# Wide products for all tiles of u, and one-hot rows of the gates from fp16 tables in PSUM

## The reference, cut to what matters

```python
def block(xc):                                   # 128 tokens of width 1024
    q = (xc @ w_q).reshape(PEER_CHUNK, PEER_HEADS, 2, half)
    sc = jnp.einsum('thpd,hpnd->thpn', q, subkeys).astype(jnp.float32)
    s1, i1 = lax.top_k(sc[:, :, 0], PEER_TOPK)
    s2, i2 = lax.top_k(sc[:, :, 1], PEER_TOPK)
    cand = (s1[..., :, None] + s2[..., None, :]).reshape(PEER_CHUNK, PEER_HEADS, ncand)
    cidx = (i1[..., :, None] * PEER_N_KEYS + i2[..., None, :]).reshape(PEER_CHUNK, PEER_HEADS, ncand)
    top, pos = lax.top_k(cand, PEER_TOPK)
    idx = jnp.take_along_axis(cidx, pos, axis=-1).reshape(PEER_CHUNK, PEER_HEADS * PEER_TOPK)
    gate = jax.nn.softmax(top, axis=-1).reshape(PEER_CHUNK, PEER_HEADS * PEER_TOPK)
    u_e = jnp.take(u, idx, axis=0)
    v_e = jnp.take(v, idx, axis=0)
    act = jax.nn.gelu(jnp.einsum('ted,td->te', u_e, xc).astype(jnp.float32))
    return jnp.einsum('te,ted->td', (gate * act).astype(v_e.dtype), v_e)
```

## Time and profile before

| | |
|---|---|
| Median of 3 runs | 2635.6 us |
| Lowest, highest | 2635.51, 2636.83 us |
| Span of the profiled execution | 2636.8 us |
| TensorE busy | 2599.8 us |
| VectorE busy | 1903.2 us |
| ScalarE busy | 1486.2 us |
| GpSimd busy | 709.0 us |
| Tiles of u of layer 0, first narrow one to the first product of v | 392.95 to 667.17 us |

### The profile page before, as it was taken

One profiled execution on the slowest core, in us unless ns is written; L12 is line 12 of the kernel. 1 busy time (PEld: TensorE's weight loads), 2 busy tenths in 40 slices (PEclk: granted clock), 3 DMA queues, 4 the chain that ended last, 5 costly groups with the idle time before them and its releaser, 6 DMA issues.

```text
span 2636.8 us, 41561 instructions
## 1 busy us (share of the span) xinstructions
PE 2599.8 (99%) x15917; PEld 2295.5 (87%) x15917; DVE 1903.2 (72%) x3327; ACT 1486.2 (56%) x2420; POOL 709.0 (27%) x354
## 2 busy tenths in 40 slices
PE   9999999999999999999999999999999999999998
PEld 7888889999888887778899998888878888998887
DVE  5667799888666667877998886666678767756784
ACT  4443567778555454655677875554454457543543
POOL 0001787777100002015886773000010021100000
PEclk9999999999999999999999999999999999999999
DMA  6555555454666665345655556666645656213564
GB/s 235 161 174 185 168 188 180 154 160 154 206 193 193 195 194 191 115 146 167 191 181 158 159 154 199 208 193 195 195 158 188 191 171 185 71 65 120 177 191 160
DMA packets 124996, 452.49 MB, mean 172 GB/s; under 512 B 13936, under 2 KB 14064, under 8 KB 124800
## 3 DMA queue, kind: packets, MB, share of 16 engines
q1 hardware_dynamic: 122832, 442.62, 53.1%
q0 software_dynamic: 1968, 7.22, 0.9%
HBM read 447.68 MB, written 2.10 MB: 171 GB/s over the span
## 4 chain that ended last, share of the span: by engine, by line
PE 93%; DVE 4%; issue 1%; ACT 1%; DMA 0%; POOL 0%; SPq 0%; DVEq 0%; POOLq 0%; ACTq 0%
PE ps L651 14%; PE ps L681 11%; PE ps L683 11%; PE ps L682 11%; PE ps L625 7%; PE ps L648 7%; PE ps L626 7%; PE ps L627 7%; PE ps L668 2%; PE ps L670 2%; PE ps L669 2%; DVE W L1758 2%; PE ps L799 2%; PE ps L941 1%; PE ps L787 1%
## 5 line engine op out<-in xcount | busy, mean ns | idle before, releaser
L1241 ACT ACTIVATE hi<-ring 128x1024 fp32r<-128x1024 f32 x830 | 866.4, 1049 | 211.2 <-PE ps L683 106.5
L2677 POOL TENSOR_TENSOR ring_r<-ring,hi 128x1024 fp32r<-128x1024 f32 x260 | 623.1, 2407 | 1131.3 <-ACT hi L1241 1131.1
L1788 DVE TENSOR_TENSOR ring_r<-ring,hi 128x1024 fp32r<-128x1024 f32 x570 | 696.8, 1228 | 256.1 <-ACT hi L1241 254.6
L625 PE MATMUL ps<-xT_r,hi 128*128 128x256 f32 x1560 | 453.0, 290 | 1.0 <-DVE ring_r L1788 1.0
L626 PE MATMUL ps<-xT_r,hi 128*128 128x256 f32 x1560 | 440.4, 282 | 0.0
L627 PE MATMUL ps<-xT_r,ring_r 128*128 128x256 f32 x1560 | 440.2, 282 | 0.0
L681 PE MATMUL ps<-hi,oht_r 128*128 128x512 f32 x1040 | 404.8, 389 | 0.3 <-DVE oht_r L1758 0.2
L682 PE MATMUL ps<-ring_r,oht_r 128*128 128x512 f32 x1040 | 404.6, 389 | 0.0
L683 PE MATMUL ps<-hi,oht_r 128*128 128x512 f32 x1040 | 404.6, 389 | 0.0
L651 PE MATMUL ps<-xT_r,hi 128*128 128x512 f32 x1600 | 383.5, 391 | 0.0
L651 PEld LDWEIGHTS ps<-xT_r,hi 128*128 128x128 f32 x1600 | 293.5, 188 | 56.5
(11 more groups left out here) (299 smaller groups left out, 3621.7 us busy)
## 6 DMA issues: line engine op xcount, KB each, us to landing
ring<-in_peer_u SPq DMA_DIRECT2D x256, 512.0 KB, 3.5
ring<-in_peer_v SPq DMA_DIRECT2D x256, 512.0 KB, 4.2
ring<-in_f SPq DMA_DIRECT2D x132, 512.0 KB, 3.6
ring<-in_ret_vg SPq DMA_DIRECT2D x32, 512.0 KB, 3.6
ring<-in_peer_q SPq DMA_DIRECT2D x32, 512.0 KB, 3.6
ring<-in_ret_qk SPq DMA_DIRECT2D x16, 512.0 KB, 3.6
ring<-in_ret_out SPq DMA_DIRECT2D x16, 512.0 KB, 3.5
ring<-in_in_shift SPq DMA_DIRECT2D x14, 512.0 KB, 3.6
```

The costliest lines, as they stand in the source:

```text
L625: pe.matmul(o, h, xT[:, k, 0:256], start=k == 0, stop=False)
L1241: hid.done(a.activation(hi[m % NH][:, :], ring[j % NR][:, :], ACT.Copy), j)
L1788: lo_v.done(v.tensor_tensor(low_part[j % NR][:, :], ring[j % NR][:, :], as32(hi[m % NH][:, :]), ALU.subtract), j)
L2677: lo_p.done(p.tensor_tensor(low_part[j % NR][:, :], ring[j % NR][:, :], as32(hi[m % NH][:, :]), ALU.subtract), j)
```

## The change

1. All 128 tiles of u of a layer are wide products (`mat_w`), each in a bank of its own. `joined` for tiles from 64 on adds the halves of both tiles of a pair into the bank of the even one; the bank of the odd one is free then, that of the even one after `weigh`.
2. The gate stretch begins at tile 64 (before 62). Tiles 80, 100 and 112 (`TWO_GATES`) carry two gate steps.
3. The picks of all 256 tokens are kept as fp16 (index digits, and the gate in two parts), and transposed at tile 63 in eight fp16 transposes into bank 7, as two tables in which values of two tokens stand side by side. VectorE reads them there.
4. The one-hot rows of four tokens are made by two VectorE operations of 1024 columns: a comparison (`equal`) of `P_iota2`, the column numbers written twice each in fp16, and a multiplication (`hot`). The rows of two tokens alternate column by column, so TensorE reads both operands at a step of two. ScalarE has no part in it.
5. `low_half` and `gelu` on ScalarE, `gated`, `joined`, `weigh` on VectorE get a new order in the gate stretch; the ones are put into W by ScalarE alone, from tile 4 on; candidate and pick buffers move from W to `oht`, `selT` and `fzt`.

```diff
-PEER_A0 = 69
+PEER_A0 = 84
-GATE_TILE = 62
-U_WIDE = 44
+GATE_TILE = 64
+PICK_TILE = 63
+EXP_TILE = (27, 57)
+TWO_GATES = (80, 100, 112)
...
+        def tables(l):
+            t = psum[bank_of["peer_pick", l]].bitcast(F16).rearrange("p (w j z s) -> p w j z s", w=2, z=2, s=2)
+            return t[:, 0], t[:, 1]
...
+        GATES, _g = {}, 0
+        for _i in range(GATE_TILE, 128):
+            GATES[_i] = [g for g in range(_g, _g + 1 + (_i in TWO_GATES)) if g < 64]
+            _g += len(GATES[_i])
...
                 def gate(g):
                     b = bank("peer_g", l, g, among=B7)
-                    pe.wait_ge(*at(dve, "spread", l, g))
-                    pe.wait_ge(*at(act, "hot", l, g))
-                    hot = P_oh[g % 2]
-                    for s in range(4):
+                    pe.wait_ge(*at(dve, "hot", l, g))
+                    equal, hot = P_equal[g % 2], P_hot[g % 2]
+                    for t in range(4):
+                        j, q = t // 2, t % 2
                         for z in range(2):
-                            ins = pe.matmul(b[:, s * 128:s * 128 + 128], hot[:, s, 2, :], hot[:, s, 1 - z, :], start=z == 0, stop=z == 1)
+                            ins = pe.matmul(b[:, t * 128:t * 128 + 128], equal[:, j, 1, :, q], hot[:, j, z, :, q], start=z == 0, stop=z == 1)
...
+                for i in range(128):
+                    if i == PICK_TILE:
+                        bank("peer_pick", l, among=(7,))
+                        pe.wait_ge(*at(dve, "picks", l, 1))
+                        for tt in range(2):
+                            for z in range(4):
+                                ins = pe.transpose(tables(l)[z // 2][:, tt * 64:tt * 64 + 64, z % 2, :], P_picks[tt][:, z, :], P_ident)
+                        mm.done(ins, "peer_pick", l)
+                    mat_w(TILE["peer_u", l * 128 + i], None, "peer_u", l, i, among=B7)
+                    for g in GATES.get(i, ()):
+                        gate(g)
...
+            def joined(l, i):
+                v.wait_ge(*at(act, "low_half", l, i))
+                to = W[:, i * 256:i * 256 + 256]
+                if i >= GATE_TILE:
+                    to = ps("peer_u", l, i - i % 2)[:, i % 2 * 256:i % 2 * 256 + 256]
+                tt_(to, ps("peer_u", l, i)[:, 0:256], low_halves[i % 4], ALU.add, name=("joined", l, i))
+                if i < GATE_TILE or i % 2:
+                    empties(dve, "peer_u", l, i)
...
+                step(v.tensor_copy, P_iota2, b3(iota, [128, 128, 2], 2))
+                step(v.tensor_copy, P_ident, ident)
...
-                    if tt:
-                        picked(0)
-                        joined_by(1.8)
...
+                    stt_(e3, e3, GATE_SCALE, b3(second[:, 0:8], [128, 8, 16], 2), ALU.mult, ALU.mult)
+                    step(v.tensor_copy, P_picks[tt][:, 2, :], P_ev)
+                    tt_(P_picks[tt][:, 3, :], P_ev, P_picks[tt][:, 2, :], ALU.subtract, name=("picks", l, tt))
...
                 def one_hots(g):
+                    v.wait_ge(*(at(mm, "peer_g", l, g - 2) if g >= 2 else at(mm, "peer_pick", l)))
+                    index, gates = (z[:, g * 2:g * 2 + 2] for z in tables(l))
+                    equal, shape = P_equal[g % 2], [128, 2, 2, 128, 2]
+                    dve.done(v.tensor_tensor(equal, P_iota2.unsqueeze(1).unsqueeze(1).broadcast_to(shape), index.unsqueeze(3).broadcast_to(shape),
+                                             ALU.is_equal), "equal", l, g)
+                    v.wait_ge(dve.sem, dve.n)
+                    dve.done(v.tensor_tensor(P_hot[g % 2], equal[:, :, 0].unsqueeze(2).broadcast_to(shape), gates.unsqueeze(3).broadcast_to(shape),
+                                             ALU.mult), "hot", l, g)
...
+                for i in range(GATE_TILE, 127):
+                    for g in GATES[i]:
+                        gated(g)
+                        if g == GATES[i][0]:
+                            joined(l, i)
+                        if g < 62:
+                            one_hots(g + 2)
+                    if not GATES[i]:
+                        joined(l, i)
+                    if i % 2 == 0 and i > GATE_TILE:
+                        weigh(i - 2)
```

More of the change, by code:

```diff
@@ L800, in gate @@
                     mm.done(ins, "peer_g", l, g)
[L802 to L810, removed]
-                        for j in range(i, i + 2):
-                            mat_w(TILE["peer_u", l * 128 + j], None, "peer_u", l, j, among=B7)
-                        continue
-                    g = i - GATE_TILE
-                    mat_t([TILE["peer_u", l * 128 + i + j] for j in range(2)], None, "peer_u", l, i, among=B7,
-                          behind=(lambda j: gate(g + j)) if 0 <= g < 64 else None)
+                for i in range(128):
[9 more added lines that the diff above has]
+                        gate(g)
@@ L1396, in peer @@
                 prep(1)
+                low_half(127)
                 gelu(126)
@@ L2062, in topk @@
                         joined_by(2.35)
-                        red_(P_picks[tt][z], eq, ALU.add)
+                        with nc.allow_low_precision(reason="an index is a whole number under 128"):
+                            red_(P_picks[tt][:, z, :], eq, ALU.add)
                         joined_by(2.35)
@@ L2114, in prep, with gated @@
                     dve.done(v.tensor_tensor(hi_part[:, 256:512], Wv[:, k, :], as32(hi_part[:, 0:256]), ALU.subtract), "prep", l, k)
-                one_hots(0)
-                one_hots(1)
-                step(v.memset, W[:, P_ONES[-1][1] * 256:], 1.0)
-                v.wait_ge(*at(act, "ones", l))
-                v.wait_ge(*at(act, "gelu", l, GATE_TILE - 2))
-                for g in range(64):
+                def gated(g):
                     wg = Wv[:, :, g * 4:g * 4 + 4]
@@ L2126, in peer @@
                     empties(dve, "peer_g", l, g)
-                    if g < 62:
-                        one_hots(g + 2)
-                    if g % 2 == 0 and g:
-                        weigh(GATE_TILE + g - 2)
-                empties(dve, "peer_iota", l)
-                for i in range(GATE_TILE + 62, 126, 2):
-                    weigh(i)
+                for i in range(first, GATE_TILE - 1):
+                    joined(l, i)
+                one_hots(0)
+                one_hots(1)
+                joined(l, GATE_TILE - 1)
+                v.wait_ge(*at(act, "ones", l))
+                v.wait_ge(*at(act, "gelu", l, GATE_TILE - 2))
+                for i in range(GATE_TILE, 127):
[6 more added lines that the diff above has]
+                    if not GATES[i]:
+                        joined(l, i)
+                    if i % 2 == 0 and i > GATE_TILE:
+                        weigh(i - 2)
+                empties(dve, "peer_pick", l)
                 prep(0)
                 prep(1)
+                joined(l, 127)
                 weigh(126)
@@ L2715, in peer @@
                     split(TILE["peer_u", l * 128 + i] + 2)
-                gains(l, 0, mm, "peer_u", l, 126)
+                gains(l, 0, mm, "peer_u", l, 127)
                 if l:
```

118 lines of the change are left out of this document (38 added, 80 removed).

## The result

The changed kernel takes 2748.8 us (median of 4 runs, 2747.2 to 2749.6) against 2636.1 us for the kernel before on the same chip: **1.0422 times as long, 95% interval 1.0410 to 1.0435, 112.6 us more.** The forecast was 2719 us, so the direction and the mechanism came out and some 29 us were missing. The profiled execution has a span of 2745.4 us.

A forecast was written before the change was run, and what follows sets the result against it. TensorE, busy 99% of the span, was taken to set the time. Net bank waits 72.0 us, late top-k 6.6 and clock 5 summed to 83.6 us on the 2635.6 us median, giving 2719 us, range 2698 to 2825.

The forecast's parts named there:

- Waits for banks: Gate stretch: TensorE waits 0.77 us at every second gate, 5.2 and 3.55 us around two-gate tiles; 43.9 us a layer.
- Narrow tiles to wide, with transposes and gates: u tiles: 84 a layer turn wide, saving 16.3 us in all; extra transposes cost 0.2 us a layer, gate matmuls nothing.
- Top-k late: Before tile 63's transposes: SBUF operations slowed beside GpSimd, 0 to 1.45 us each; 3.3 us a layer on path, 6.6 in all.
- Clock: TensorE's clock may drop after the 5.2 us waits: three drops of 1.7 us, 5 us taken, bounds 0 and 20.
- VectorE's steps from a gate's start to a free bank: Even gates: the bank is free 4.05 us after the gate's first matmul, while TensorE wants it after 3.28.
- the totals fit and do not decide: VectorE per gate and tile: 2.8 us of work against TensorE's 3.28 us fits, but totals do not decide.
- ScalarE's splitting as covered: Top-k stretch: exponentials hold up ScalarE's splitting of u, but it runs two tiles ahead of TensorE, more than the delay.
- The gate matmuls: TensorE's gates: reading both operands at a step of two changes nothing; cost bounded at 0.5 us a gate.
- Rival 3: Gate matmuls: strided weights load slowly, a gate takes 1.0 us instead of 0.5, +30 us a layer, 2780 us; 8%.
- 3.28 us for a gate and a tile: Gate stretch: TensorE takes 0.50 us for a gate plus 2.78 for a wide tile.
- rival 2: VectorE's one-hots run at one result per cycle, 1.21 us each, so waits grow 47 us a layer, 2813 us; 18%.
- rival 1: Gate stretch: no bank comes late, so the wide tiles' gain shows and the kernel is faster, 2620 us; 4%.

The follow-up runs named there:

- the eighth: Changed kernel with tiles and gates in separate banks, early table copies, and scaled gates written to PSUM (also listed as number 8): 2623.5 us, 0.9952 of the kernel before.
- Experiments 1: Changed kernel with VectorE's weigh of a pair moved ahead of the next even tile's gated: 2649.1 us, 1.0047 of the kernel before.
- experiment 2: Changed kernel with u tiles in banks 0 to 4 and gates in 5 and 6 from tile 64, nothing moved: 2640.3 us, 1.0012 of the kernel before.
- 5: Changed kernel with two gates at tile 80 alone, one each at tiles 100 and 112: 2707.6 us.
- experiment 6: Changed kernel without the second one-hot operation, the scaling by the gates, so its output differs: 2699.8 us.
- experiment 3: Changed kernel with idle TensorE transposes filling its six long waits of each layer: 2728.5 us, 20.2 us less.
- experiment 4: Changed kernel with the two table copies moved from the top-k's start into the queries' products: 2742.1 us, 6.7 us less.

## Why the prediction was right, and where 29 us were missing

| Term | Forecast | Measured |
|---|---|---|
| Waits for banks | +87.8 | +87.3 |
| Narrow tiles to wide, with transposes and gates | -15.9 | -12.8 |
| Top-k late | +6.6 | +14 |
| Clock | +5 | +23 |
| Sum | +83.6 | +111.5 |

The whole kernel shows +112.6; the last 1 us is in no row. The second row is measured as the way from the first product on u to the first on v in the kernel before (397.2 us in each layer) and in the eighth (390.8), where no wait of this change is left.

**The banks** were right to the half microsecond. Measured are 23 waits of 0.74 us, and three times 5.27 and 3.61 us a layer by the starts in the timeline (520.71 less 514.54 and 0.90 us for two gates; 532.28 less 528.23 and 0.44), 43.7 us against 43.9. For VectorE's steps from a gate's start to a free bank the prediction had 4.05 us: `weigh` ends 4.01 us behind the gate at 462.89, and the next gate starts 0.05 us later, 4.06 in all. Experiments 1 and 2 show it is the bank and nothing else, 5 and 6 that its size is the sum of those steps. Since the two engines wait for each other in turn, no busy share could show it; the forecast's remark that the totals fit and do not decide was the right one.

**The clock** is the step that failed, as a mis-sized term. The prediction saw that the waits of 5.2 us "could each bring" a drop, set 0 to 20 us, and took three drops of 1.7 us, 5 in all. Eleven of the twelve long waits brought one, five of the six of 3.4 us too, and experiment 3 puts them at 20.2 us, 1.7 for each of the twelve on the mean. That is the upper bound that the text had itself worked out from the earlier trace rows; the price of one drop was right, their number was not. No row spoke for three. Two more drops stand behind the waits at the transposes: from there to the first gate it is 7.46 and 7.60 us in the two layers, against 6.07 in both layers of the eighth kernel, which has neither wait nor drop there. That makes 2.9 us, and 23 in all.

**The top-k** was the other mis-sized term. The list of steps was right, and so was the mechanism, with its upper bound of 1.45 us for an operation: 8.7 us a layer. The value taken, 3.6, was near the middle of a range without a reason for the middle. In layer 0 the two copies cost 4.3 us too much and the cast and subtraction of the first half 2.2. Three of these four exceed the bound of 1.45 for one operation (the copies take 2.51 and 2.31 us, the subtraction 2.39, where some 0.3 would do), since an operation can wait for nearly the whole of a GpSimd instruction. From the first product on u to the transposes it is 182.4 us in each layer of the changed kernel and 175.5 in the eighth: 7.0 a layer, 14 in all. Of each 7.0 us, 4.2 are spent at the transposes, where the forecast had 3.3. The other 2.8 lie ahead of them, where the forecast had nothing: it named ScalarE's splitting as covered, since it runs two tiles ahead, and it was not. The waits for GpSimd at L663 came out of it, and experiment 4 removed them.

**The gate matmuls** cost no more with steps of two: eight take 0.63 us to the end of the last and 0.44 to the next start, against 0.62 and 0.43 before (542.61 to 543.04 in the kernel before). Rival 3 is out. The forecast's 3.28 us for a gate and a tile was 0.03 short of the 3.32 and 3.31 us that alternate in experiment 2. The forecast had taken the cost of a gate, 0.50 us, from narrow tiles; behind a gate a wide tile takes 2.88 us in place of 2.78, a narrow one 2.95 in place of 2.88. Over 128 gates this makes 4 us; forecast and measured value of the table's second row lie 3.1 us apart.

**One result per cycle**, rival 2, is out by the rows at L2079 and L2082: 0.68 and 0.69 us for 1024 columns. Both operations read an fp16 operand from PSUM. By the tier table of the Trainium skill's VectorE: DVE Perf Modes they would have gone at one per cycle; section 5.1 of the Trainium skill's Vector Engine (DVE) Microarchitecture Reference allows two, and these rows agree with that. **The fast case**, rival 1, did not come in this kernel, but nearly its number did in the eighth: 2623.5 us, where rival 1 had 2620, or 2624 with the 4 us just named. So the direct gain of the wide tiles is real, and 125 us of waits and half clock lay on top of it.

## What to carry to other kernels

When buffers go round in a ring, count for each one how many takes lie between its content's last reader and the next take, again for each place where the pattern slips; a product that takes a bank where it took half of one shortens the ring for everybody. A pool apart for what lives long cost nothing here and moved 108 us. Price a wait of TensorE of some 3 us or more at its length plus 1.7 us of half clock (the mean of twelve, which lay between 0 and 2.4). Price a VectorE cast or copy wholly in SBUF, or an operation with two sources there, beside a busy GpSimd at up to one GpSimd instruction (2.4 us here), unless one operand can be put in PSUM.

## What the runs showed of the hardware

- In the changed kernel TensorE's clock fell to 1.2 GHz behind eleven of the twelve waits of 3.4 and 5.1 us (behind one of 3.4 in layer 1 the tile took 2.9 us), and behind none of the 46 of 0.74 us. In experiment 6 it fell behind all six waits of 3.63 us and three of the six of 2.70, so one and the same wait can bring a drop or not. In experiments 1, 2 and 8, with no wait over 1.3 us in the gate stretch, it stayed at 1.00 there. 42 idle transposes in a wait kept it at 2.4 GHz.
- A VectorE comparison and a multiplication with one fp16 operand in PSUM, another in SBUF, values in adjacent pairs and otherwise repeated, ran at 1024 columns in 0.68 and 0.69 us, as long as 512 columns of fp32 take.
- A cast of 128 columns within SBUF took 0.38, 1.88 or 1.90 us with GpSimd at work, and 0.29 us out of PSUM. By where in GpSimd's instruction it fell: it ended each time within 0.1 us or so behind the end of one. MAX8 within SBUF was not held up (0.30 us).
- fp16 matmuls of 128 columns with both operands at a step of two start 0.055 us apart (0.44 us for eight with the next start), no slower than packed ones (0.43).
